# TensorE waits for its own first unit before it starts the second one of each feed-forward layer

## The reference

```python
def conv_glu_ffn(h, w_up, conv_w, conv_b, w_down):      # layers 0, 1 and 6
    z = h @ w_up                                        # 1024 -> 2 * 2816
    z1 = shift_prev(z)
    z2 = shift_prev(z1)
    z = conv_w[0] * z2 + conv_w[1] * z1 + conv_w[2] * z + conv_b
    gate, val = jnp.split(z, 2, axis=-1)
    return (jax.nn.silu(gate) * val) @ w_down           # 2816 -> 1024

def swiglu(h, w13, w2):                                 # layers 2 to 5
    a, b = jnp.split(h @ w13, 2, axis=-1)
    return (jax.nn.silu(a) * b) @ w2
```

## Time and profile before

| | |
|---|---|
| median of 3 executions | 2210.74 us |
| lowest, highest | 2204.43, 2230.14 us |
| profiled execution: its own time | 2224.99 us |
| profiled execution: span from the first to the last instruction | 2223.2 us |
| busy: PE, PEld, DVE, ACT, POOL | 99%, 95%, 65%, 52%, 21% |
| mean granted TensorE clock | 0.974 of full speed |
| moved by DMA | 438.91 MB, mean 197 GB/s |

### The profile page before, as it was taken

How to read it: one execution, slowest core, us unless ns; L and a number is a source line. 1 busy time by engine, 2 the same in 40 slices (tenths; PEclk the granted TensorE clock), 3 DMA queues, 4 the chain that set the end, 5 groups by cost and what they waited for, 6 DMA issues and landing times.

```text
span 2223.2 us, 46909 instructions
## 1 busy us (share of the span) xinstructions
PE 2193.4 (99%) x18966; PEld 2122.5 (95%) x18966; DVE 1445.1 (65%) x1981; ACT 1157.8 (52%) x1579; POOL 470.9 (21%) x246
## 2 busy tenths in 40 slices
PE   9999999999999999999999999999999999999998
PEld 8888999999999999997999999998999999999998
DVE  5453788765888699875676589957533254557554
ACT  6511555665656544575544454457544455556664
POOL 0011000100000145403144434410144300001443
PEclk9968999999999999999999999999999999999999
DMA  7220466543566578552588588744355453444552
GB/s 264 96 47 2 153 254 243 192 175 134 215 258 245 192 304 335 217 215 94 208 314 315 199 317 322 283 178 152 119 186 187 170 192 133 168 169 158 188 193 109
DMA packets 64388, 438.91 MB, mean 197 GB/s; under 512 B 7127, under 2 KB 9848, under 8 KB 12170
## 3 DMA queue, kind: packets, MB, share of 16 engines
q1 hardware_dynamic: 60480, 430.75, 52.4%
q10 hardware_dynamic: 3786, 6.38, 1.3%
HBM read 434.49 MB, written 2.62 MB: 197 GB/s over the span
## 4 chain that ended last, share of the span: by engine, by line
PE 92%; ACT 3%; DVE 3%; issue 1%; POOL 0%; DMA 0%; DVEq 0%; ACTq 0%
PE ps L346 25%; PE ps L347 24%; PE ps L348 24%; ACT w_hi L284 1%; PE ps L360 1%; PE ps L362 1%; PE ps L368 1%; PE ps L498 1%; PE ps L484 1%; PE ps L1636 1%; PE ps L388 1%; PE ps L389 1%; PE ps L390 1%; PE ps L1658 1%; DVE w_lo L290 1%
## 5 line engine op out<-in xcount | busy, mean ns | idle before, releaser
L346 PE MATMUL ps<-h_hi,w_hi 128*128 128x256 f32 x3412 | 961.2, 282 | 3.9 <-DVE h_lo L1546 3.0
L347 PE MATMUL ps<-h_lo,w_hi 128*128 128x256 f32 x3412 | 954.9, 280 | 0.0
L348 PE MATMUL ps<-h_hi,w_lo 128*128 128x256 f32 x3412 | 954.8, 280 | 0.0
L290 DVE TENSOR_TENSOR w_lo<-ring,w_hi 128x2048 fp32r<-128x2048 f32 x272 | 623.4, 2293 | 401.7 <-ACT w_hi L284 397.8
L284 ACT ACTIVATE w_hi<-ring 128x2048 fp32r<-128x2048 f32 x334 | 638.6, 1913 | 153.1 <-PE ps L348 147.9
L346 PEld LDWEIGHTS ps<-h_hi,w_hi 128*128 128x128 f32 x3412 | 646.9, 190 | 9.7 <-issue 4.9
L348 PEld LDWEIGHTS ps<-h_hi,w_lo 128*128 128x128 f32 x3412 | 650.0, 190 | 0.0
L347 PEld LDWEIGHTS ps<-h_lo,w_hi 128*128 128x128 f32 x3412 | 645.8, 189 | 0.2
L346 PE MATMUL ps<-g_hi,w_hi 128*128 (+1 forms) x1232 | 343.7, 279 | 1.2 <-POOL g_lo L894 0.9
L347 PE MATMUL ps<-g_lo,w_hi 128*128 (+1 forms) x1232 | 343.4, 279 | 0.0
L348 PE MATMUL ps<-g_hi,w_lo 128*128 (+1 forms) x1232 | 343.4, 279 | 0.0
(11 more groups left out here) (482 smaller groups left out, 2661.2 us busy)
## 6 DMA issues: line engine op xcount, KB each, us to landing
ring<-in_weights SPq DMA_DIRECT2D x334, 1024.0 KB, 4.8
mix<-in_modw SPq DMA_DIRECT2D x72, 1024.0 KB, 4.9
bias_rows<-below_mix ACTq DMA_DIRECT2D x1, 1536.0 KB
mix<-in_c_ssd ACTq DMA_DIRECT2D x1, 1536.0 KB, 8.5
x<-in_x SPq DMA_DIRECT2D x2, 512.0 KB, 4.1
ring<-in_weights SPq DMA_DIRECT2D x2, 512.0 KB, 6.3
mix<-in_c SPq DMA_DIRECT2D x2, 512.0 KB, 5.7
mix<-bias_rows ACTq DMA_DIRECT2D x1, 1024.0 KB, 6.1
```

The source lines that it names most:

```text
L290: dve.tensor_tensor(w_lo[:, n % SLOTS], ring[:, n % SLOTS], w_hi[:, n % SLOTS], ALU.subtract).then_inc(lo_ready[n % SLOTS], 1)
L346: pe.matmul(o, w[0], a_hi, start=first, stop=False, **kw)
L347: pe.matmul(o, w[0], a_lo, start=False, stop=False, **kw)
L348: return pe.matmul(o, w[1], a_hi, start=False, stop=last, **kw)
```

## The change

TensorE's up unit m = 1 gets one more wait, ahead of that for `lo_ready`: for `unit_done` at the value n, where n is the number of the unit that it is about to compute. That is the point at which the last matmul of up 0 is complete. Nothing else differs. It occurs seven times, once in each feed-forward layer.

```diff
             def up(m, n, i):
+                if m == 1:
+                    pe.wait_ge(unit_done, n)
                 if m >= 2:
                     if conv:
                         pe.wait_ge(z_free, zbase[name] + m - 1 + i * 2)
```

## The result

The changed kernel takes 2224.45 us (median of 20 executions, 2202.64 to 2238.94), the kernel before beside it 2207.02 us (20 executions, 2191.15 to 2230.14). The ratio is 1.007, 95% interval 1.0043 to 1.0097: slower by less than one per cent, some 9 to 21 us, where I forecast 10 us less. The profiled execution takes 2224.55 us. This ratio and all later ones leave out the executions that lie more than 1.5% above the fastest of their kernel, which in a kernel that scatters by 2% takes out ordinary ones too, so where it matters I add the difference of the means of all executions.

A forecast was written before the change was run, and what follows sets the result against it. TensorE was taken to bound the kernel: 2225.0 us profiled, plus 2.2 for the drains, minus 27.0 for four long layers turning short, plus 0.4 for end stalls, gives 2200.6 us; the 8-in-10 range was 2195 to 2230.

The forecast's parts named there:

- What bounds the kernel: Whole span: TensorE has matmuls in flight for 99%; each layer keeps one pace, about 117.8 or 113.3 ns per matmul.
- The price of the drain: At up 1 of each feed-forward layer: the wait, attached to the weight load, loses 0.32 us, 2.2 us for seven.
- The other form: At up 1, if the sequencer's own instruction carries the wait: 0.38 us each, 2.7 us in all, as upper bound.
- The clock: At the new gap, TensorE idle some 0.06 us: the clock stays at 1.00, nothing counted.
- the ten of eleven: Restarts in PE's timeline: ten of 11 lead into the short pace, so four long layers become short, gaining 27.0 us.
- the one at 468.8 us: Restart that loads the activations as weights: the only one of 11 leading into the long pace.
- The scatter of the kernel before: Three executions of the kernel before: one, two and five long layers at 6.7 us above 2198, pace drawn anew each execution.
- The end stalls: Ahead of the last down unit in layers 0 and 1: each stall grows by 0.2 us, 0.4 us lost in both.
- B: Rival, feed-forward layers: pace redrawn without preference, 2 to 5 of seven long, 2220 us (2212 to 2234); chance 0.18.
- A: Rival, feed-forward layers: only the drain, layers keep their pace, current time plus 2.2 us, 2213 for the median; chance 0.10.
- C: Rival, at up 1: the restart always leads to the long pace, layers 2, 4, 6 lose 20.3, 2247.5 us; chance 0.11.
- D: Rival, at up 1: the wait doesn't hold since the value is there, 2211 us; chance 0.03 together with unforeseen.

The follow-up runs named there:

- sequencer_form_every: Kernel before plus the wait behind that for `lo_ready` at every feed-forward unit but up 0, meant for the queue's own instruction: 2305.7 us, 1.0409.
- drain_every_unit: Kernel before plus the change's wait ahead of every feed-forward unit but the first of each layer, 224 waits: 2333.48 us, 1.0559 to the kernel before.
- drain_twice_again: Repeat of the kernel with the change's wait ahead of both up 1 and up 2, against the kernel before: 2218.63 us, 1.0024.
- drain_twice: Kernel before plus the change's wait ahead of up 1 and once more ahead of up 2 in each layer, first run: 2226.49 us, 1.007.
- sequencer_form: The change's seven waits placed behind that for `lo_ready`, so the queue's own instruction carries them, against the kernel before: 2213.58 us, 1.005.
- small_at_three: Kernel before plus one unused 16-column matmul ahead of each of up 1, 2 and 3, no new wait: 2208.21 us, 0.9998.
- before_third: The kernel before, unaltered, run again as a control against itself: 2205.6 us, 0.9973.
- after_again: The changed kernel, unaltered, run a second time against the kernel before: 2223.54 us, 1.0041.
- small_matmuls: Kernel before plus three unused 16-column matmuls ahead of up 1 in each feed-forward layer, no new wait: 2223.01 us, 1.0073.
- wide_matmuls: Kernel before plus two unused 256-column matmuls ahead of up 1 in each feed-forward layer, no new wait: 2221.09 us, 1.0069.
- one_small_matmul: Kernel before plus one unused 16-column matmul ahead of up 1 in each feed-forward layer, no new wait: 2217.9 us, 1.0072; repeated, 2215.73 us, 1.0025.

## Why the prediction was wrong

**What bounds the kernel**: right. TensorE bounds it before and after, and the layer's time is the count of its matmuls times one of two paces, held for the whole stream.

**The price of the drain**: right. The text had 0.34 us in place of 0.12, then 0.22 in place of 0.12; measured over the changed kernel's profiles 0.333 to 0.339, and 0.221 to 0.229. That is 0.32 to 0.33 us each and 2.3 for seven, where the text had 2.2. The wait is attached to the weight load, as argued. The other form measured 0.425 and 0.193, 0.38 us each, the upper bound of the text.

**The clock**: right, 1.00 in all seven windows.

**The step that failed** is "By the ten of eleven, the four layers with the long pace take the short one". It was worth 27.0 us of gain (27.2 by its own factors, since 175.5 x (1 - 113.2/117.7) is 6.7 and not 6.6). In the profile after three layers were long, two of which had been short. Two things were wrong with it. First, the eleven restarts of one trace are not eleven independent draws. Five of them stand behind the attention scores, and at these places the short pace follows 92 times of 95 over the 19 profiles; the one at 468.8 us, which went against the rule, leads to the long pace 19 times of 19. These are properties of the places. And the stall of layer 1 ahead of the last down unit, on which the argument leaned most, led to the short pace 10 times and to the long one 8 times in the 18 other profiles. Second, the pace ahead of the restart counts, which I never put beside the pace behind it. In four profiles of the changed kernel, where up 0 had settled, this restart led from short to long 9 times of 9 and from long to short 7 times of 7. The same wait turned the pace over 112 times of 112 in the loop of sequencer_form_every, 55 times of 55 in drain_every_unit and 12 of 12 in drain_twice_again, and 0 times of 12 in the one profiled execution of drain_twice. So, with that execution as the exception, it doesn't send the layers one way; it turns each over.

**What that makes of the time.** Inverting costs only if the short pace is the commoner one ahead of it. In layers 0, 1, 2 and 6, over the 19 profiles of all kernels, up 0 was short 50 times of 76, 65.8%. Without the wait 34.2% of these layers run long, with it 65.8%: 4 x 0.316 = 1.26 layers more, at 6.7 us 8.5 us. With 2.3 us for the drains, and 0.4 less for the end stalls, which are shorter in long layers, that is 10.4 us. The share has an error of 0.054, which is 2.9 us by the same sum. Over all executions of all calls the changed kernel has a mean of 2224.3 us (55 executions; one of 6178.79 us is left out) and the kernel before 2210.8 (201): 13.5 us, with a standard error of some 1.5. Compared within each call, it is 14.2, 13.2, 16.8 and 17.6 us, 15.4 with an error of 1.7. So the two agree within one and a half errors, and a rest of a few us may have another cause.

The profiles themselves count fewer long layers than that: 13 of 28 in the four of the changed kernel against 10 of 28 in the four of the kernel before, a difference that chance alone could give. What they do show is where the time is. Take each layer from the start of the last matmul of up 0 to that of the last matmul of down 10. The seven together take 1247.5, 1228.1, 1247.6 and 1228.5 us in the kernel before and 1243.8, 1250.2, 1237.0 and 1249.8 in the changed one, 7.3 us more on average; the rest of the span takes 977.0 on average before and 976.3 after. In these profiles nothing is lost outside the layers.

The profiled execution by the same terms: layers 0, 1 and 5 give back 20.1 us, layers 4 and 6 take 13.4, the drains 2.3, and the end stalls 0.9 in layers 0 and 1 less 0.4 in layer 6, so 2225.0 would become 2221.1. It took 2224.55. The seven layers became 3.7 us shorter, close to the 3.9 of these terms, and the rest of the span went from 975.7 to 978.9 us.

**The scatter of the kernel before**: half right. "The pace is drawn anew in each execution" holds: its four profiles have 4, 1, 4 and 1 long layers. The reading of a single time as a number of long layers does not. The part of the span outside the layers lies between 972.1 and 986.4 us over the 19 profiles, which is worth two layers. With 1221.5 us for seven short layers (the shortest of each in the kernel before) and the 1.8 us outside the span, an execution without a long layer would take 2195 to 2210 us. Those that had none (sequencer_form, drain_twice and small_at_three) come out at 2204 to 2210 us when the price of their own edits is taken off. The fastest execution of the kernel before took 2185.49 us, so the rest must scatter by more than these profiles show. A stall can mislead here. This one stands in the first mixer of before_third and not in the profile of before:

```profile
PE ps L1154 <- issue: 9.9, 1, 9.9
```

But the matmuls behind it start at 153.14 us there, and at 155.12 in before, without the stall.

**The end stalls**: the sign was right, the size not. They grew by 0.43 us in layer 0 and not 0.2. The text counted 48 matmuls, those of the down unit between up 21 and the last down unit. But in layers 0 and 1 of before and after alike the last down unit starts 11.72 us behind the last matmul of up 20, and not at a fixed distance from that of up 21 (6.07 or 6.28 us). ScalarE comes to the bank of up 21 only when it is done with up 20, in layer 0 of the kernel before at 427.56 us, where the last matmul of up 21 was complete at 426.84:

```profile
427.24 0.42 ACT L820 ACTIVATE g_hi<-gf 128x256 fp32r<-128x256 f32 x1 [2.35 <-DVE gf L862]
427.56 0.58 ACT L804 ACTIVATE zs<-ps 128x512 f32<-128x512 f32 x1
```

So two units, 96 matmuls at 4.5 ns, add to the stall, 0.43 us.

**The rivals.** B, a redraw without preference with 2220 us, was nearest in time, and wrong in the mechanism: behind a settled up 0 nothing is redrawn. A, only the drain, would be 1.001; the changed kernel's four ratios are 1.007, 1.0041, 1.0093 and 1.0092. The mean of these excludes A, though after_again alone does not. C, always long, is excluded by layers 0, 1, 2 and 5 of the changed kernel. D, that the wait doesn't hold, by the distance of 0.34 us.

**What stays open.** Why drain_twice in its first profile kept the short pace over its drains at the same distance of 334 ns: in that profile the next matmuls came at 0.224, 0.114 and 0.123 us, elsewhere at 0.221, 0.118 and 0.117, so the state that inverts isn't fixed by the distance alone. In the second profile of this same program 12 waits of 12 inverted. Why small_matmuls, wide_matmuls and the first one_small_matmul were 1.007 slower, which the repetition of the last did not confirm (1.6 us over all executions, error 2.7), and where the last 4 us of small_at_three went. Whether the 5 us between 15.4 and 10.4 are one more cause or chance. And what in the engine makes two paces: no edit here touched that.

## What to carry to other kernels

Where one engine bounds the kernel, divide window lengths by counts before you price an edit: if the same instructions have two paces, a small edit can be worth its effect on the pace, here some three times its price. A rule about what restarts do has to be read from several executions and as pairs, the pace before and the pace behind; many events of one trace may be a single draw. If an engine has to be drained, measure which form of the wait leaves the pace alone, and look in the trace whether the program gives it that form everywhere: inside a loop it didn't here.

## What the hardware showed that I had not expected

A stream of fp32r matmuls of 256 columns, each with its own weight load, ran at one of two paces at full clock, 113.3 or 117.8 ns each, and kept it for 1440 to 1550 matmuls; once settled it changed only at a restart or behind a matmul of another kind put in between. A restart 333 to 339 ns behind the last matmul, released by that matmul's own completion at the weight load, inverted the pace 16 times of 16 in the changed kernel (up 0 settled), 55 times of 55 in drain_every_unit, 112 of 112 in the loop of sequencer_form_every and 12 of 12 in drain_twice_again, with one execution (drain_twice) in which it did so at none of its 12 waits. The same wait carried by the queue's own instruction, 424 to 430 ns behind, kept the short pace in 45 of 45 cases and the long one in 12 of 18. A matmul of 16 columns in between kept the short pace 25 times of 25 and turned the long one into the short one 9 times of 15, for 0.22 us. And the same program, on one core, spreads over 2185 to 2244 us from one execution to the next; between one and four long layers at 6.7 us each, as its four profiles had, are 20 of those 59 us.
